# Other planner costs and thresholds for the modulation steps of a two-block kernel

## The chip, the cores and the metric

One Trainium2 chip, one core. The metric is the device time of one execution in microseconds (us). The engines are TensorE (PE, with its weight loads shown as PEld), VectorE (DVE), ScalarE (ACT), GpSimd (POOL) and SyncE (SP), which issues the transfers.

## The reference, cut to what matters

256 tokens of 1024 columns go through two blocks. The first mixes an mLSTM and a sparse attention (an indexer picks 64 keys for a query), with sigmoid and silu gates on the mLSTM's output, and ends in a gated residual and a norm. The second has two layers; the first layer's mixer is MLA attention, the second's is MoBA. Each layer is modulated by a small vector that depends on the input `c` alone:

```
c_act = silu(c)
mod = (c_act @ mod_w[i] + mod_b[i]).reshape(B, 6, D)[:, :, None, :]
hin = x * (1.0 + mod[:, 1]) + mod[:, 0]        # into the mixer
x = layer_norm(ALPHA * x + mod[:, 2] * y)
hin = x * (1.0 + mod[:, 4]) + mod[:, 3]        # into the feed-forward part
x = layer_norm(ALPHA * x + mod[:, 5] * y)
```

A product of one row with a 1024 x 1024 matrix per vector, six vectors for each layer. The vectors 0, 1, 3 and 4 of a layer are needed as columns, before the mixer (0, 1) and before the feed-forward part (3, 4). The vectors 2 and 5 are made on TensorE by other steps (`mod_k`).

## The kernel before

Weights stream from HBM in tiles of 128 x 1024 ("units", 512 KB). Each is split into a high and a low part: ScalarE rounds it (step `hi`), VectorE subtracts (step `lo`), and TensorE makes three products in place of one (lines 1291 to 1293). All engines work through one list of steps, each in the order of that list; an engine skips what isn't its own. The list is made by the function `order()` when the program is built.

`order()` keeps two clocks. `clock["pe"]` is the sum of `cost_pe` over the steps so far, and `clock["ve"]` is the end of VectorE's work, which never lies before the TensorE clock and grows by `cost_ve`. Their difference is called the backlog here: how far VectorE lags by the planner's own costs. The costs are numbers in a table, in units meant as microseconds.

The columns of the modulation come from a generator, `modulation()`. For each vector, in the order (0,0), (0,1), (0,3), (0,4) of the first layer (layer, vector), and then the same of the second, it gives these turns:

- eight steps `mod_v` (k from 0 to 7): a transfer of a 512 KB tile and a VectorE multiply and add over 128 x 1024 into an accumulator (lines 1612 and 1614)
- two turns that do nothing (one in the second layer)
- `mod_one`, eight short matmuls that sum over the partitions (line 1386), and `mod_sum`, a ScalarE copy of the sum from PSUM (line 2164)
- `mod_pe`, two transposes on TensorE (line 1395) that wait for `mod_sum`, and `mod_fin`, small VectorE operations (from line 1628)

So twelve turns make one vector. A turn is taken at the end of a weight unit, and between the heads of an attention that is being finished, where this holds:

```
t[2] = float(clock["ve"] - clock["pe"] < -t[1] and clock["pe"] - clock["mod"] > MOD_APART)
```

`-t[1]` is the threshold: `MOD_PACE[0]` in the first block, `MOD_PACE[1]` from the key and value projections of MLA on. `MOD_PACE[2:]` are positive and are rates, not thresholds; they hold after the first layer's MLA. What is missing when a vector is needed is placed at once, all in one go, by `until(i, m)` at the head of `modulated(...)`, which is called ahead of the transposes that feed a mixer or a feed-forward part.

Four stretches of the list matter here. The projections `w_aqk`, `w_av` and `w_az` (units with these names) run beside the mLSTM and the indexer. The projection `w_moz` (16 units) runs beside the sparse attention, whose steps are `sc` and `norm` with the task name "dsa" (lines 1804, 1823, 1826; TensorE's transposes of line 1471 wait for them); in it lie `gate_mo` (lines 1853 and 1859) and `ev_mz` (1866 and 1870). Then come `w_out`, `w_ple` and `w_gate`. Last, MLA: `mla_uv`, `mla_uk`, `mla_uq`, and `mla_o`.

The end of `mla_o` is the first layer's residual and layer norm. For each half t of the tokens VectorE adds and takes statistics (lines 1978 to 2010), POOL takes a power (2490), and ScalarE, with VectorE for a part of t = 1, scales (step `ln_fin`: lines 2350, 2356 and 2018). Then `modulated(0, 1)` is called: `until(0, 4)`, then five `mod_k` of another vector (line 1377), the transposes of t = 0 (1305), one `mod_k`, the transposes of t = 1, the scaling by the modulation's columns (1572 on VectorE, 2129 on ScalarE), and the feed-forward matmuls.

Of the kernel before, what the change touches and what calls it, by code (L numbers as in the profile page):

```python
# [20 lines left out]
CONST_AT, NCONST = spans(CONSTS)  # L21


MOD_PACE, MOD_APART = [-4.0, -5.0, 0.4, 0.5, 0.5], 2.0
LSTM_PACE, DSA_PACE, MLA_PACE, MOBA_PACE, GATES_PACE, INDEXER_PACE = 1.05, 1.53, 1.6, 0.87, 0.6, 0.8
SHARE = 0.65

# [30 lines left out]
def cost_ve(kind, a):  # L58

    wide = {"ix_s": 0, "ix_k": 0, "dist": 0}  # L60
    if kind in wide:
        return {"ix_s": 0.75, "ix_k": 1.5, "dist": 0.6}[kind] * (1.0 + 0.3 * a[0])
    if kind in ("lo", "hi") or kind in ("ev_mv", "ev_av", "ev_k", "ev_v", "ev_q"):
        return 0.0 if kind == "hi" or a[4 if kind in ("lo", "ev_v") else 2 if kind in ("ev_av", "ev_q") else 3] != "V" \
            else 1.2 if kind == "lo" else 0.65
    if kind in ("sc", "norm"):
        return 0.47 if of(a[0], a[1])[1] else 0.35
    if kind == "ml_s":
        return 0.95 if a[1] else 1.3
    if kind == "tab":  # L70
        return (0.6, 0.9, 1.5, 1.2, 1.9)[a[0]]
    return {"lo_half": 0.65, "xt_s": 0.9, "xt_hl": 0.65, "xf": 0.25, "xt_m": 1.0, "xt_lo": 0.65, "mod_v": 1.25,
            "mod_row": 0.4, "mod_pe": 0.2, "mod_fin": 0.6, "gev": 0.7, "gate": 0.55, "ix_f": 0.5, "conv": 2.7,
            "silu": 0.7, "ml_o": 0.5, "ev_az": 0.65, "fin_dsa": 1.1, "fin_o": 0.43, "ev_mz": 2.0, "gated": 1.7,
            "ev_wo": 0.65, "pt2": 0.65, "ev_gate": 1.3, "rms2_r": 0.5, "gain": 1.25, "res_m": 0.65, "res_a": 0.65,
            "res_s": 0.65, "ev_cq": 0.8, "rope": 0.85, "ffn_a": 1.8, "ffn_g": 0.65}.get(kind, 0.0)

# [22 lines left out]
def of(task, i):  # L100

    return (i // 4 * 2 + i % 2, i // 2 % 2) if task == "dsa" else (i // 2, i % 2)
# [42 lines left out]
def order():  # L145
# [5 lines left out]
    def add(*step):  # L151
        steps.append(step)
        clock["pe"] += cost_pe(step[0], step[1:])
        clock["ve"] = max(clock["ve"], clock["pe"]) + cost_ve(step[0], step[1:])
# [2544 lines left out]
```

## Time and profile before

| what | value |
| --- | --- |
| time, median of 3 runs | 877.66 us (877.63 to 877.71) |
| the profiled execution's own time | 876.84 us |
| its span, first to last instruction | 875.0 us |
| TensorE busy | 849.9 us, 97% |
| VectorE busy | 670.3 us, 77% |
| ScalarE busy | 457.8 us, 52% |
| mean granted TensorE clock | 0.998 |

Busy time is the union of an engine's instructions. A row of the timeline has the start, the length, the engine, the line, the operation and the tiles; in brackets, how long the engine had been idle before it, and what released it. The profiled execution took 0.82 us less than the median of the runs.

### The profile page before, as it was taken

Reading aid. Unit: us, or ns where it says so; the run is one execution under the profiler, and the core shown is the slowest. Engines: PE = TensorE matmul, PEld = TensorE weight load, DVE = VectorE, ACT = ScalarE, POOL = GpSimd, SP = SyncE. Lnnn points to the kernel's source line nnn. Section 1 sums busy time; section 2 is a strip of 40 time slices with the busy share of each in tenths; the row PEclk is TensorE's granted clock in tenths of the full one; section 3 lists DMA queues with packets and bytes.
Section 4 is the critical chain, followed back from the end, with each engine's and each line's share of the span. In section 5 each row is a group of like instructions: output and inputs, shape, how many; then the busy total and the mean of one; then the engine's idle time right before and its main releaser. Section 6 shows DMA issues by size and latency. Waiting matters only on the chain. (4 is left out here: it accounts for less than half of the span.)

```text
span 875.0 us, 14595 instructions
## 1 busy us (share of the span) xinstructions
PE 849.9 (97%) x5778; PEld 747.4 (85%) x5778; DVE 670.3 (77%) x1096; ACT 457.8 (52%) x737; POOL 81.4 (9%) x77
## 2 busy tenths in 40 slices
PE   9999999899999999999999999999999999999996
PEld 9989987677776987799999999689976999999995
DVE  6698798997887887799568767797777876566567
ACT  6564555554556545575544454365553854454450
POOL 1100004100001110012201000100000101001011
PEclk9999999999999999999999999999999999999999
DMA  9856654576885751989757796288617976646501
GB/s 336 308 178 222 197 210 148 201 243 217 310 337 190 292 197 35 403 318 360 263 164 270 284 366 201 95 289 336 220 69 302 328 292 198 209 146 201 185 1 49
DMA packets 56773, 200.61 MB, mean 229 GB/s; under 512 B 6585, under 2 KB 7793, under 8 KB 56705
## 3 DMA queue, kind: packets, MB, share of 16 engines
q1 hardware_dynamic: 55664, 196.43, 63.4%
q0 software_dynamic: 1040, 3.24, 1.2%
q8 instruction: 46, 0.75, 0.3%
q14 instruction: 23, 0.18, 0.1%
HBM read 198.50 MB, written 1.08 MB: 228 GB/s over the span
## 5 line engine op out<-in xcount | busy, mean ns | idle before, releaser
L1291 PE MATMUL ps<-XT,wsp 128*128 128x256 f32 x760 | 215.0, 283 | 2.2 <-issue 1.6
L1292 PE MATMUL ps<-XT,wsp 128*128 128x256 f32 x760 | 212.0, 279 | 0.0
L1293 PE MATMUL ps<-XT,wsp 128*128 128x256 f32 x760 | 211.9, 279 | 0.0
L1527 DVE TENSOR_TENSOR wsp<-ring,wsp 128x1024 fp32r<-128x1024 f32 x131 | 160.3, 1230 | 13.3 <-ACT wsp L2101 13.3
L2101 ACT CAST wsp<-ring 128x1024 fp32r<-128x1024 f32 x131 | 136.1, 1047 | 58.0 <-PE ps L1293 52.8
L1291 PEld LDWEIGHTS ps<-XT,wsp 128*128 128x128 f32 x760 | 142.7, 188 | 5.5 <-issue 3.6
L1292 PEld LDWEIGHTS ps<-XT,wsp 128*128 128x128 f32 x760 | 142.6, 188 | 0.5
L1293 PEld LDWEIGHTS ps<-XT,wsp 128*128 128x128 f32 x760 | 142.6, 188 | 0.0
L1291 PE MATMUL ps<-wsp,ra 128*128 128x512 f32 (+1 forms) x256 | 97.7, 382 | 2.9 <-DVE ra L1842 2.1
L1293 PE MATMUL ps<-wsp,ra 128*128 128x512 f32 (+1 forms) x256 | 97.2, 380 | 0.0
L1292 PE MATMUL ps<-wsp,ra 128*128 128x512 f32 (+1 forms) x256 | 96.6, 377 | 0.0
L1513 DVE SCALAR_TENSOR_TENSOR wk<-ps,cols,wk 128x255 f32<-128x255 f32 (+1 forms) x88 | 36.3, 475 | 70.9 <-ACT wk L2395 70.9
L1527 DVE TENSOR_TENSOR wsp<-arena,wsp 128x1024 fp32r<-128x1024 f32 x72 | 88.6, 1238 | 1.5 <-ACT wsp L2101 1.5
L2101 ACT CAST wsp<-arena 128x1024 fp32r<-128x1024 f32 x72 | 75.1, 1045 | 24.7 <-PE ps L1293 20.5
L1291 PE MATMUL ps<-XT,ra 128*128 128x256 f32 x288 | 81.3, 282 | 0.0
L1292 PE MATMUL ps<-XT,ra 128*128 128x256 f32 x288 | 80.7, 280 | 0.0
L1293 PE MATMUL ps<-XT,ra 128*128 128x256 f32 x288 | 80.7, 280 | 0.0
L1291 PE MATMUL ps<-wsp,XT 128*128 128x512 f32 x180 | 74.1, 412 | 3.6 <-issue 2.2
L1292 PE MATMUL ps<-wsp,XT 128*128 128x512 f32 x180 | 71.2, 396 | 0.0
L1293 PE MATMUL ps<-wsp,XT 128*128 128x512 f32 x180 | 71.1, 395 | 0.0
L2508 POOL TENSOR_TENSOR ra<-wk,ra 128x512 fp32r<-128x512 f32 x22 | 40.7, 1850 | 306.6 <-ACT ra L2408 306.6
L1291 PEld LDWEIGHTS ps<-wsp,ra 128*128 128x128 f32 x256 | 48.1, 188 | 15.0 <-DVE ra L1842 3.5
(276 smaller groups left out, 1538.3 us busy)
## 6 DMA issues: line engine op xcount, KB each, us to landing
ring<-in_mod_w SPq DMA_DIRECT2D x48, 512.0 KB, 4.8
arena<-in_mod_w SPq DMA_DIRECT2D x45, 512.0 KB, 6.5
ring<-in_ffn_o SPq DMA_DIRECT2D x29, 512.0 KB, 4.7
ring<-in_ffn_a SPq DMA_DIRECT2D x26, 512.0 KB, 4.7
arena<-in_ffn_b SPq DMA_DIRECT2D x25, 512.0 KB, 5.5
ring<-in_ffn_b SPq DMA_DIRECT2D x19, 512.0 KB, 4.9
arena<-in_ffn_a SPq DMA_DIRECT2D x18, 512.0 KB, 5.4
arena<-in_ffn_o SPq DMA_DIRECT2D x15, 512.0 KB, 5.1
```

Source lines behind the costliest of these rows:

```text
L1291: pe.matmul(o, l[0], r[0], start=start, stop=False)
L1292: pe.matmul(o, l[0], r[1], start=False, stop=False)
L1293: return pe.matmul(o, l[1], r[0], start=False, stop=stop)
L1513: ve.scalar_tensor_tensor(o[:, sh:256], src[:, q * 256:(q + 1) * 256 - sh], scale(tap, q), o[:, sh:256], MUL, ADD).then_inc(*done("V", top ...
L1527: ve.tensor_tensor(w[:, 1024:1024 + n], raw[slot[0]][:, 0:n], w[:, 0:n].bitcast(f32), SUB).then_inc(*done("V", "lo", u, also=[("raw", *slo ...
L2101: ac.copy(parts[p[0]][:, 0:n], raw[slot[0]][:, 0:n]).then_inc(*done("A", "hi", u))
L2508: po.tensor_tensor(gp[g[0]][:, 512:1024], wk[s[0]], gp[g[0]][:, 0:512].bitcast(f32), SUB).then_inc(*done("G", "ffn_lo", i, u, also=[("wk", ...
```

## The change

Two thresholds rise (from 4 to 5, and from 5 to 7), and entries of the planner's VectorE table change: `sc` and `norm` of the sparse attention cost 0.15 more each, `ev_mz` costs 1.4 in place of 2.0, and `gate_mo` costs 1.6. Until now `gate_mo` had no entry of its own, and cost 0: the entry stood under the name "gated", which no step bears. No instruction is added or removed; the order of the steps is what can change.

```
-MOD_PACE, MOD_APART = [-4.0, -5.0, 0.4, 0.5, 0.5], 2.0
+MOD_PACE, MOD_APART = [-5.0, -7.0, 0.4, 0.5, 0.5], 2.0
...
     if kind in ("sc", "norm"):
-        return 0.47 if of(a[0], a[1])[1] else 0.35
+        return (0.47 if of(a[0], a[1])[1] else 0.35) + (0.15 if a[0] == "dsa" else 0.0)
...
-            "silu": 0.7, "ml_o": 0.5, "ev_az": 0.65, "fin_dsa": 1.1, "fin_o": 0.43, "ev_mz": 2.0, "gated": 1.7,
+            "silu": 0.7, "ml_o": 0.5, "ev_az": 0.65, "fin_dsa": 1.1, "fin_o": 0.43, "ev_mz": 1.4, "gate_mo": 1.6,
```

## Rows read from the trace of the kernel before

**Rows 1.** The page, busy time by engine: us, share of span, instructions.

```profile
PE 849.9 (97%) x5778; PEld 747.4 (85%) x5778; DVE 670.3 (77%) x1096; ACT 457.8 (52%) x737; POOL 81.4 (9%) x77
```

**Rows 2.** Busy time in windows: PE, PEld, DVE, ACT, POOL, granted clock, DMA share, GB/s.

```profile
150.00:165.00 15.00, 14.16 (x77) 9.76 (x77) 14.28 (x30) 6.44 (x17) 2.41 (x4) 1.00 0.60 207
165.00:180.00 15.00, 12.89 (x71) 9.22 (x70) 13.47 (x33) 8.49 (x24) 1.48 (x2) 1.00 0.38 129
```

**Rows 3.** Timeline of TensorE, the rows before which it was idle, 100 to 240 us.

```profile
126.84 0.38 PE L1291 MATMUL ps<-XT,wsp 128*128 128x256 f32 x1 [0.58 <-DVE wsp L1527]
...
164.26 0.33 PE L1471 MATMUL ps<-cst,pb 128*128 128x128 f32 x1 [0.84 <-DVE pb L1826]
166.32 0.50 PE L1291 MATMUL ps<-wsp,XT 128*128 128x512 f32 x1 [0.32 <-DVE wk L1866]
169.61 0.33 PE L1471 MATMUL ps<-cst,pb 128*128 128x128 f32 x1 [1.04 <-DVE pb L1826]
175.91 0.70 PE L1457 MATMUL ps<-arena 64*128 64x256 f32 x4 [0.75 <-DVE ra L1564]
```

**Rows 4.** Timeline of VectorE, 113 to 177 us.

```profile
113.83 1.28 DVE L1614 SCALAR_TENSOR_TENSOR R<-ring,cactr,R 128x1024 f32<-128x1024 f32 x1
...
134.04 1.28 DVE L1614 SCALAR_TENSOR_TENSOR R<-ring,cactr,R 128x1024 f32<-128x1024 f32 x1
...
138.53 0.29 DVE L1804 CUSTOM_DVE_ANT_0 pb<-ps,arena 128x128 f32<-128x128 f32 x1 [2.01 <-POOL arena L2457]
...
146.49 0.17 DVE L1628 TENSOR_TENSOR small<-ps,cols 128x8 f32<-128x8 f32 x1 [0.75 <-PE ps L1395]
147.12 0.29 DVE L1804 CUSTOM_DVE_ANT_0 pb<-ps,arena 128x128 f32<-128x128 f32 x1 [0.47 <-PE ps L1457]
...
149.66 0.88 DVE L1859 SCALAR_TENSOR_TENSOR arena<-arena,small 128x256 f32<-128x256 f32 x2
...
162.11 1.27 DVE L1614 SCALAR_TENSOR_TENSOR R<-ring,cactr,R 128x1024 f32<-128x1024 f32 x1
...
176.81 1.28 DVE L1614 SCALAR_TENSOR_TENSOR R<-arena,cactr,R 128x1024 f32<-128x1024 f32 x1
```

**Rows 5.** Timeline of VectorE in MLA, 295 to 359 us.

```profile
295.23 1.28 DVE L1614 SCALAR_TENSOR_TENSOR R<-ring,cactr,R 128x1024 f32<-128x1024 f32 x1
303.43 0.42 DVE L2035 TENSOR_TENSOR wk<-ps,arena 128x256 f32<-128x256 f32 x1 [0.59 <-PE ps L1293]
304.87 0.42 DVE L2035 TENSOR_TENSOR wk<-ps,arena 128x256 f32<-128x256 f32 x1 [0.69 <-PE ps L1293]
...
345.40 0.42 DVE L1842 TENSOR_TENSOR ra<-ps,ra 128x256 fp32r<-128x256 f32 x1 [2.41 <-ACT ra L2291]
...
358.21 0.69 DVE L1978 TENSOR_TENSOR wk<-ps,R 128x512 f32<-128x512 f32 x1 [2.94 <-PE ps L1293]
```

**Rows 6.** Timeline of TensorE and ScalarE around the end of MLA, 354 to 369 us.

```profile
354.54 0.64 PE L1386 MATMUL ps<-R,cst 128*32 128x256 f32 x8
355.25 0.37 ACT L2164 COPY msum<-ps 128x256 f32<-128x256 f32 x1 [1.24 <-PE ps L1386]
...
360.80 0.38 PE L1395 MATMUL ps<-cst,msum 128*128 128x128 f32 x2
361.11 2.37 PE L1377 MATMUL ps<-arena,cactr 128*32 128x256 f32 x40
...
364.58 1.09 ACT L2356 ACTIVATE X<-X,small 128x256 f32<-128x256 f32 x2
...
365.00 1.27 PE L1305 MATMUL ps<-cst,X 128*128 128x128 f32 x8
365.99 0.56 ACT L2129 ACTIVATE wk<-ps,small 128x256 f32<-128x256 f32 x1 [0.32 <-DVE small L1649]
...
368.09 0.36 PE L1291 MATMUL ps<-XT,wsp 128*128 128x256 f32 x1 [0.81 <-issue]
```

**Rows 7.** Timeline of TensorE, its longest idle time inside the run.

```profile
266.38 1.09 PE L1305 MATMUL ps<-cst,X 128*128 128x128 f32 x8 [1.59 <-DVE X L1965]
```

**Rows 8.** Timeline of TensorE, the longest idle time in MLA's attention.

```profile
340.52 0.33 PE L1471 MATMUL ps<-cst,pb 128*128 128x128 f32 x1 [0.76 <-DVE pb L1826]
```

## The prediction

> **What bounds the kernel.** I read the page's busy times first: TensorE is busy for 849.9 of 875.0 us [rows 1], so about 25 us of idle time are all that an order of steps can win, and anything that stops TensorE is paid in full. Then the list of TensorE's idle rows, to see which of them the modulation's steps can reach. Up to the end of MLA (about 368 us) the change moves steps; behind it the thresholds are rates that stay as they are, and the list must come out the same. In the reachable part the idle rows are few: 0.58 us in `w_az`, and 0.84, 0.32, 1.04 and 0.75 us beside the sparse attention, 2.95 us in sum [rows 3]. There VectorE is the late one: it is busy 14.28 and 13.47 of 15 us in the windows that hold them, and TensorE 14.16 and 12.89 [rows 2]. The longest in MLA's attention is 0.76 us [rows 8]. So the most that could be won is some 3 to 4 us. Last I read the timeline around the end of MLA, because there the modulation's leftovers are placed in one go.
>
> **What the change moves.** The new table is nearer to the trace: `gate_mo` is one operation over 512 columns and two over 256, and the two alone take 0.88 us [rows 4], where the old table had 0. A higher cost in the sparse stretch and a higher threshold pull in opposite directions, so I followed the backlog by the planner's table: the old list gives the value (in the planner's units) at each chance, and I carried the differences.
>
> In `w_aqk` the chance at unit 4 had 4.18, and is now taken; the next one rises to 3.83 + 1.25 = 5.08 and is refused. From there the steps k = 5, 6, 7 of vector (0,0) come one chance earlier each, and the last one moves from the end of `w_az` to `w_av`. So (0,0) is finished one turn earlier, and the first three `mod_v` of (0,1) come at `w_moz` units 3, 4 and 5 in place of 4, 5 and 6. Then the new costs bite. The backlog at units 6 to 13 comes out as 5.99, 7.97, 7.30, 7.13, 6.11, 5.64, 6.53, 5.81, all over 5: no turn. Unit 14 has 4.81, one turn. The old list took eight `mod_v` of (0,1) in `w_moz`, the new one takes four. From `w_out` to `w_gate` all chances are taken in both lists. After `w_gate` the old list had seven `mod_v` of (0,3), the new one has three: it goes into MLA four turns late.
>
> In MLA the old list took 16 turns and left one (`mod_pe` with `mod_fin`) for `until(0, 4)`. The new one needs 21. With threshold 7 it takes 18: one old refusal (the spacing) is gone since `mod_one` now lies ahead of it, one with backlog 5.39 passes; the chance after `mla_o` unit 3 has 7.82 and is refused, and one stays refused for spacing. So three turns are left for `until(0, 4)`: a blank one, `mod_one` with `mod_sum`, and `mod_pe` with `mod_fin`. Two more turns would have to be found for `mod_one` to be placed in time, so this doesn't hang on one narrow comparison.
>
> **Cost at the end of MLA.** In the old list `mod_one` ran at 354.54 and ScalarE's copy at 355.25, six us ahead; `mod_pe` started at 360.80, directly behind the last matmul of `mla_o`, and from there TensorE went on without a gap: five `mod_k`, the transposes, the second half of them at 365.00 [rows 6]. In the new list `mod_one` stands behind that last matmul, and `mod_sum` stands on ScalarE behind `ln_fin` of both halves. The last of these ends at 364.58 + 1.09 = 365.67 [rows 6]. I take 0.5 us off, since `mod_one` (0.64) no longer lies ahead of the last matmuls, and VectorE waited for these (2.94 us idle) [rows 5, 6]: 365.2. The copy takes 0.37, so `mod_pe` starts at 365.6 in place of 360.80. Everything queued behind it on TensorE waits too, and it is just the work that used to fill the layer norm: 4.20 us from `mod_pe` to the second half of the transposes (365.00 less 360.80). These start at 369.8, the scaling some 0.6 us later at 370.4 against 365.99, so 4.4 us are lost, and the first feed-forward matmul goes from 368.09 to about 372.5. Nothing hides it: the whole of TensorE's queue stands behind `mod_pe`, and VectorE's and ScalarE's next steps behind the scaling. Bounds: 3.9 us if the scaling starts with the first pair of transposes at once, 5.3 us without the 0.5 and with the same distance of 0.99 us as before.
>
> **The other terms.** (1) `w_av` to `w_az`: one `mod_v` of 1.28 us more stands ahead of the low parts (113.83 and 134.04 are where the old k = 6 and 7 lie) [rows 4], and TensorE already waits 0.58 us for one of these [rows 3]. Between 0, if the small idle times of VectorE take it, and +1.28; I take +0.6. VectorE gets it back at 134, ahead of a wait of 2.01 us for POOL [rows 4], where less work is worth nothing. (2) The sparse stretch: up to 164 us VectorE has the same three `mod_v` ahead, a unit earlier each, which can only use its idle 0.75 + 0.47 us at 146 to 147 [rows 4]. The steps that leave the stretch are those from 176.81 on [rows 4], and behind 175.91 TensorE had no wait there [rows 3]: that relief comes too late. Gain between 0 and all 2.95 us; I take 1.0, near the idle time that can be used. (3) Early MLA: four `mod_v` (5.1 us) come in from 297 us on, and three leave by 317. VectorE had waited 0.59 and 0.69 us for TensorE there [rows 5], so it wasn't behind; the backlog reaches 4.3. Between 0 and +1.3 (5.1 less the 3.8 of the three that leave); I take +0.3. (4) Late MLA: three `mod_v` come in after `mla_o` unit 1, where VectorE has 2.41 and 2.94 us idle [rows 5]. Between 0 and +1.3, the first of them ahead of work that TensorE waits for; I take 0, since three times 1.28 are 3.8 us and the two idle times are 5.35. (5) `w_out` to `w_gate` has the same seven `mod_v` in both lists: 0. The transfers move with the `mod_v`, same count and bytes; no wait of TensorE in rows 3 is for one.
>
> Sum: 4.4 + 0.6 - 1.0 + 0.3 + 0 = +4.3 us. On the profiled execution that is 876.84 + 4.3 = 881.1 and a span of 879.3; the runs shown have a median 0.82 higher, so 877.66 + 4.3 = 882.0 us; I say 881.9.
>
> **The clock.** No row here has TensorE below its full granted clock: the windows have 1.00, and the longest idle time inside the run is 1.59 us [rows 2, 7]. The forecast makes a gap of 365.6 less about 361.0, that is 4.6 us, nearly three times that. If the clock fell to 1.2 GHz in it, the 4.20 us of matmuls and transposes behind it would take up to 4.2 us more. The Trainium skill says on the page "TensorE: Matmul & The Clock Gate", section "Part 1: The HAM clock gate (the "warmup" mystery)", that an idle array falls back to the half rate and needs sustained work to return; by that rule this gap is of the kind that can cost more than its length. The trace neither shows nor excludes it.
>
> **Rivals.** The clock falls in the new gap: up to 4.3 + 4.2, about 884 to 886.5 us. For it: such a gap is new here. Against: none in rows. Chance 0.07.
>
> MLA stalls as well: three more `mod_v` late in MLA and a backlog of 7.82 make the matmuls of `mla_o` wait. One late `mod_v` reaches TensorE twice, or the layer norm starts later by 1 to 3 us: 883.5 to 886. Against it: the idle 2.94 us just ahead of the norm [rows 5]. Chance 0.09.
>
> The end costs little: the copy doesn't wait for the norms, or `until(0, 4)` has only `mod_pe` left, as before. Then terms 1 to 4 alone are left, -0.1 us, and with a better half of the sparse stretch -1: 876.7 to 879.3, no change. Chance 0.11.
>
> Faster: the sparse stretch was bound by VectorE through the modulation, and pulling steps out of it takes away all 2.95 us and the 0.58 us in `w_az`, while the end costs nothing: 874.2 to 875.8. It decides only where at most `mod_pe` is left at the end, since 3.53 is less than 4.4. Chance 0.08.
>
> The forecast, +2 to +6: chance 0.65.
>
> **How the numbers follow.** 0.2% of the time, 1.75 us, is about what a measurement of this kernel can tell. Slower: 0.65 + 0.07 + 0.09 = 0.81, of which 0.01 may fall below the bound; same 0.11 + 0.01 = 0.12; faster 0.08. The range leaves out the faster case (0.08), part of the no-change one, and the upper part of the two dear ones: 878.4 to 884.8. The likeliest case's own range is 880 to 883.8.
>
> **What would show it.** In the changed kernel's trace: line 1386 with eight matmuls directly behind the last `mla_o` matmul, near 360 us; line 2164 on ScalarE behind line 2356's second group; an idle time of TensorE of 4 to 5 us before line 1395, ended by the copy; behind it the same distances as before. Beside the sparse attention only one row of line 1614 (or 1612) between 160 and 195 us, and idle rows of TensorE of about 2 us in sum in place of 2.95. Four more rows of line 1614 between 290 and 307 us. Behind 370 us, everything the same and later. It would be wrong if line 1386 stands inside `mla_o`, or if the idle rows of MLA's attention grow by over 1 us.

## The result, and the profile after

The changed kernel takes 883.72 us (median of 5 runs, 883.27 to 884.87), the kernel before 877.63 us beside it: a ratio of 1.0074, 95% interval 1.0062 to 1.0085, so slower by 6.1 us. The forecast was 881.9, range 878.4 to 884.8. The profiled execution took 883.27 us, the fastest of the five; its span is 881.4 us, 6.4 more than before.

The page's busy times are those of before [rows 1]: the same instructions, the same work.

```profile
PE 850.1 (96%) x5778; PEld 747.4 (85%) x5778; DVE 670.8 (76%) x1096; ACT 458.0 (52%) x737; POOL 79.1 (9%) x77
```

TensorE's idle rows up to the last projection of MLA, to be read against [rows 3, 7, 8]:

```profile
116.20 0.70 PE L1448 MATMUL ps<-arena,pb 128*128 128x257 f32 x2 [1.31 <-DVE pb L1773]
129.08 0.39 PE L1291 MATMUL ps<-XT,wsp 128*128 128x256 f32 x1 [0.47 <-DVE wsp L1527]
...
161.43 0.44 PE L1471 MATMUL ps<-cst,pb 128*128 128x128 f32 x2 [0.44 <-DVE pb L1826]
170.87 0.33 PE L1471 MATMUL ps<-cst,pb 128*128 128x128 f32 x1 [1.03 <-DVE pb L1826]
177.16 0.70 PE L1457 MATMUL ps<-arena 64*128 64x256 f32 x4 [0.74 <-DVE ra L1564]
...
309.18 0.49 PE L1464 MATMUL ps<-arena 128*128 128x128 f32 x2 [0.90 <-POOL arena L2502]
...
341.19 0.33 PE L1471 MATMUL ps<-cst,pb 128*128 128x128 f32 x1 [0.76 <-DVE pb L1826]
```

The differences here are small: beside the sparse attention the idle times add up to 2.21 us in place of 2.95, and there is one new wait of 1.31 us in the mLSTM's stretch and one of 0.90 us in early MLA. The end of MLA is another matter. The timeline of the same kernel, to be read against [rows 6]:

```profile
360.79 0.64 PE L1386 MATMUL ps<-R,cst 128*32 128x256 f32 x8
...
364.48 1.09 ACT L2356 ACTIVATE X<-X,small 128x256 f32<-128x256 f32 x2
365.47 0.35 ACT L2164 COPY msum<-ps 128x256 f32<-128x256 f32 x1
365.88 0.69 PE L1395 MATMUL ps<-cst,msum 128*128 128x128 f32 x2 [4.45 <-ACT msum L2164]
366.50 3.67 PE L1377 MATMUL ps<-arena,cactr 128*32 128x256 f32 x40
...
371.69 1.09 PE L1305 MATMUL ps<-cst,X 128*128 128x128 f32 x8
...
372.38 0.56 ACT L2129 ACTIVATE wk<-ps,small 128x256 f32<-128x256 f32 x1 [6.56 <-PE ps L1305]
...
374.48 0.36 PE L1291 MATMUL ps<-XT,wsp 128*128 128x256 f32 x1 [0.70 <-issue]
```

`mod_one` (1386) now stands behind the last matmul of `mla_o`, its copy (2164) behind the layer norm of both halves (2356), and TensorE idles 4.45 us before `mod_pe` (1395). Then comes what the forecast had only as a rival: the five `mod_k` take 3.67 us in place of 2.37, and the short transposes 0.69 in place of 0.38. The windows of 2 us of the changed kernel show why; the number behind the five busy times is the granted clock:

```profile
362.00:364.00 2.00, 0.00 (x0) 0.00 (x0) 1.52 (x5) 1.27 (x2) 0.45 (x1) 1.00 1.04 414
364.00:366.00 2.00, 0.12 (x1) 0.13 (x2) 0.73 (x2) 1.64 (x4) 0.11 (x1) 0.95 1.03 393
366.00:368.00 2.00, 2.00 (x18) 0.95 (x22) 0.84 (x5) 0.00 (x0) 0.00 (x0) 0.50 1.03 408
368.00:370.00 2.00, 2.00 (x28) 0.82 (x20) 0.00 (x0) 0.00 (x0) 0.00 (x0) 0.70 0.78 315
370.00:372.00 2.00, 2.00 (x23) 1.33 (x20) 0.00 (x0) 0.00 (x0) 0.00 (x0) 1.00 0.04 16
```

A granted clock of 0.50 is TensorE's lower level, 1.2 GHz. It fell while the engine stood idle, and was back when it had worked for some 3 us. All five executions of the changed kernel have a mean granted clock of 0.994 to 0.996, where the kernel before has 0.997 or more, which fits such a fall in each of them; only the profiled one shows where.

**Where the time went.** All kernels here run the same 1614 groups of three weight matmuls in the same order. So the start of the n-th matmul of line 1293 in one trace can be set against the n-th in another: the difference is how far a kernel lags. Worked out from the profiled executions (us, minus: ahead of before; the experiments are told below):

| kernel | at 48 | 130 | 187 | 302 | 349 | 372 | 867 us of before |
| --- | --- | --- | --- | --- | --- | --- | --- |
| changed | 0.46 | 2.24 | 1.23 | 0.39 | 0.66 | 6.39 | 6.39 |
| gap kept busy | 0.24 | 2.02 | 1.02 | 0.21 | 0.51 | 4.83 | 5.09 |
| mod_one hoisted | 0.22 | 1.94 | 0.83 | 0.00 | 0.27 | 0.42 | 0.56 |
| before, mod_one late | 0.38 | 0.31 | 0.19 | 0.25 | 0.27 | 7.13 | 7.46 |
| new thresholds alone | 0.41 | 2.21 | 6.56 | 5.56 | 5.79 | 4.81 | 4.96 |
| new costs alone | 0.24 | 0.31 | -0.92 | -2.29 | -1.89 | 6.53 | 6.45 |
| mod_pe behind the transposes | 0.15 | 1.97 | 1.00 | 0.21 | 0.50 | 1.56 | 1.79 |
| hoisted, 4 in w_aqk | 0.39 | 0.48 | 0.44 | -0.37 | -0.06 | 0.09 | 0.46 |
| none beside sparse | 0.59 | 2.46 | -0.80 | -2.86 | -0.66 | 5.48 | 5.54 |
| between the rows | 0.52 | 0.56 | -0.66 | -2.02 | -1.63 | -0.97 | -0.79 |

At 48 us no step has moved yet, and every kernel is 0.15 to 0.59 behind: the profiled execution of before had a lucky start (it was also 0.8 us under its median). With that taken off, the changed kernel has lost 0.66 - 0.46 = 0.2 us when the second half of `mla_o` begins. Between 349 and 372 us it loses 5.73 us, and from there to the end nothing. One thing to know when reading the table: while only one of two kernels has run a step that moved, the step itself shows as a lag; `mod_one` makes up to 0.8 us of it.

### The profile page after: what moved, and what is told of

Same layout as the page of the kernel before. It is cut to its first block and busy times, and to the rows that moved or that the text cites. A ratio compares the mean times of both kernels' runs of the same rounds, so it can differ in the third digit from the quotient of the medians.

```text
span 881.4 us, 14596 instructions
## 1 busy us (share of the span) xinstructions
PE 850.1 (96%) x5778; PEld 747.4 (85%) x5778; DVE 670.8 (76%) x1096; ACT 458.0 (52%) x737; POOL 79.1 (9%) x77
## 5 line engine op out<-in xcount | busy, mean ns | idle before, releaser
L1527 DVE TENSOR_TENSOR wsp<-ring,wsp 128x1024 fp32r<-128x1024 f32 x128 | 157.3, 1238 | 15.1 <-ACT wsp L2101 15.0
L2101 ACT CAST wsp<-ring 128x1024 fp32r<-128x1024 f32 x128 | 133.3, 1046 | 51.6 <-PE ps L1293 47.1
L2101 ACT CAST wsp<-arena 128x1024 fp32r<-128x1024 f32 x75 | 78.3, 1045 | 36.8 <-PE ps L1293 29.9
L1527 DVE TENSOR_TENSOR wsp<-arena,wsp 128x1024 fp32r<-128x1024 f32 x75 | 91.3, 1223 | 0.5 <-ACT wsp L2101 0.5
```

Source lines behind the costliest of these rows:

```text
L1527: ve.tensor_tensor(w[:, 1024:1024 + n], raw[slot[0]][:, 0:n], w[:, 0:n].bitcast(f32), SUB).then_inc(*done("V", "lo", u, also=[("raw", *slo ...
L2101: ac.copy(parts[p[0]][:, 0:n], raw[slot[0]][:, 0:n]).then_inc(*done("A", "hi", u))
```

## The experiments

**1. The gap kept busy.** The changed kernel, but the late `mod_one` writes its sums seven times over.

```
-                    for j in range(4):
+                    for j in list(range(4)) * (7 if (i, m) == (0, 4) else 1):
                         ins = pe.matmul(ps[b[0]][32 * j:32 * j + 32, 0:256], ones[:, 0:32],
```

> The changed kernel with the eight short matmuls of the late mod_one repeated seven times (same values written again), so that TensorE works through most of the 4.45 us in which it stood idle. Theory A (two costs at the end of MLA: the wait for ScalarE's copy, and the clock that falls in the gap): the wait stays, line 1395 starts as late as now, the granted clock stays at 1.00 and the 5.8 us from mod_pe to the second half of the transposes go back to 4.2, so the time falls by 1.6 us to about 882.1. Theory B (the work behind the gap is slow for another reason, the transfers or the row order): nothing but the repeated matmuls changes, 883.7 us or more.

Measured: 881.87 us, 1.0053 (1.0036 to 1.0070). Its timeline, and the window behind the gap:

```profile
360.63 3.23 PE L1386 MATMUL ps<-R,cst 128*32 128x256 f32 x56
365.72 0.44 PE L1395 MATMUL ps<-cst,msum 128*128 128x128 f32 x2 [1.86 <-ACT msum L2164]
366.09 2.37 PE L1377 MATMUL ps<-arena,cactr 128*32 128x256 f32 x40
...
369.98 1.09 PE L1305 MATMUL ps<-cst,X 128*128 128x128 f32 x8
```

```profile
366.00:368.00 2.00, 2.00 (x38) 1.20 (x40) 0.84 (x5) 0.00 (x0) 0.00 (x0) 1.00 1.02 403
```

`mod_pe` starts as late as in the changed kernel (365.72 against 365.88), but the five `mod_k` are back at 2.37 us, and from `mod_pe` to the second half of the transposes it takes 4.26 us in place of 5.81. More work for TensorE made the kernel faster, by 1.55 us there: the clock is a cost of its own, and the wait is the rest. Theory A. The trace carries this more than the times do: there are four executions, the intervals of the two kernels overlap, and one of the four took 883.65 us with a mean granted clock of 0.996 (the others 881.03 to 881.92 with 0.998), so the clock did not stay up every time.

**2. mod_one hoisted.** The changed kernel with two turns taken ahead of the last two units of `mla_o`.

```
         with_heads(0, mt)(cb, q)
+        if (cb, q) == (1, 2):
+            next(mod[0][0])
+            next(mod[0][0])
```

> The changed kernel with the blank turn and mod_one with mod_sum placed ahead of the last two units of mla_o, everything else as it is. Theory A (the loss is mod_one behind the last matmul): no wait for the copy, no fall of the clock, and the end of MLA as before the change; the time falls by 5.7 us to 878.0, that is 0.5 us above before, which is what the earlier moves lost. Theory B (the moved mod_v steps burden VectorE, and the late mod_one only shows where it falls behind): the layer norm ends later and half or less of the loss comes back, 880.5 us or more.

Measured: 877.41 us beside 877.48, ratio 1.0000 (0.9991 to 1.0010). All moved `mod_v` stand where the change put them, and the whole loss is gone; in the table the lag stays at 0.42 at 372 us. So the `mod_v` steps moved into late MLA cost nothing by themselves.

**3. Before, with mod_one late.** The opposite: the kernel before, no turn from the second half of `mla_o` on.

```
         with_heads(0, mt)(cb, q)
+        if (cb, q) == (1, 0):
+            mod[0][1] = 0
```

> The kernel before with one thing of the change: no turn from the second half of mla_o on, so that only mod_one with mod_sum (and blank turns) move behind the last matmul of mla_o. All mod_v stand where they stood. Theory A: this alone costs 5.7 us (4.1 of wait and 1.6 of clock), 883.3 us. Theory B (the loss comes from the mod_v steps moved into MLA): at most 1 us, 878.6.

Measured: 884.03 us, 1.0072 (1.0057 to 1.0087). This one displacement makes a loss as large as the whole of it. Timeline and windows of this kernel:

```profile
365.47 0.69 PE L1397 MATMUL ps<-cst,msum 128*128 128x128 f32 x2 [4.45 <-ACT msum L2166]
366.09 4.50 PE L1379 MATMUL ps<-arena,cactr 128*32 128x256 f32 x40
...
372.28 1.09 PE L1307 MATMUL ps<-cst,X 128*128 128x128 f32 x8
```

```profile
364.00:366.00 2.00, 0.53 (x2) 0.29 (x2) 0.48 (x2) 1.39 (x4) 0.00 (x0) 0.52 1.04 404
366.00:368.00 2.00, 2.00 (x21) 0.99 (x24) 0.84 (x5) 0.00 (x0) 0.00 (x0) 0.50 1.03 406
368.00:370.00 2.00, 2.00 (x28) 0.79 (x16) 0.00 (x0) 0.00 (x0) 0.00 (x0) 0.50 0.59 234
```

The gap is again 4.45 us, but the clock fell earlier in it (0.52 already in the window from 364) and stayed low for longer: 6.81 us from `mod_pe` to the second half of the transposes, where the changed kernel has 5.81. The price of the fall isn't fixed by the length of the gap; here it was 6.81 - 4.20 = 2.6 us. It is seen in one execution of each, and needn't be a difference between the kernels: their times overlap (883.22 to 884.29 us here, 883.27 to 884.87 for the changed kernel).

**4. New thresholds alone.** The kernel before with the old costs.

```
-MOD_PACE, MOD_APART = [-4.0, -5.0, 0.4, 0.5, 0.5], 2.0
+MOD_PACE, MOD_APART = [-5.0, -7.0, 0.4, 0.5, 0.5], 2.0
```

> The kernel before with the two thresholds raised (5 and 7) and the old costs. By the planner the turns then run ahead: mod_one of (0,4) falls after unit 1 of mla_o, and nothing is left for the end. Theory A: no gap at the end; what is left is the wait of 1.31 us in w_aqk, that both share, and more waits beside the sparse attention since mod_v comes in at w_moz 8 to 11, 0 to 3 us: 878 to 881. Rival: the higher thresholds are the cause of the loss whatever the costs, 883 or more. Rival: running ahead is free and early MLA gains, 877 or less.

Measured: 878.90 us (878.01 to 881.80 over 10 runs), 1.0020 (1.0011 to 1.0030); its profiled execution has a span of 880.0. It was the slowest of the ten; five took 878.01 to 878.57, with a mean granted clock of 0.997 in place of its 0.992. No gap at the end, as the planner said. But beside the sparse attention TensorE idles 0.45 + 0.69 + 0.32 + 1.04 + 0.38 + 1.51 = 4.39 us, and in the last of these the clock falls to 0.50, here too. Timeline and window of this kernel:

```profile
177.58 0.44 PE L1471 MATMUL ps<-cst,pb 128*128 128x128 f32 x2 [0.38 <-DVE pb L1826]
179.53 1.23 PE L1457 MATMUL ps<-arena 64*128 64x256 f32 x4 [1.51 <-DVE ra L1564]
180.69 0.79 PE L1291 MATMUL ps<-wsp,XT 128*128 128x512 f32 x1
181.28 0.63 PE L1292 MATMUL ps<-wsp,XT 128*128 128x512 f32 x1
```

```profile
178.00:180.00 2.00, 0.49 (x3) 0.50 (x4) 1.90 (x3) 1.77 (x4) 0.00 (x0) 0.81 0.35 139
180.00:182.00 2.00, 2.00 (x7) 1.16 (x5) 2.00 (x5) 0.04 (x1) 0.00 (x0) 0.50 0.18 18
```

The matmuls take 0.63 us in place of 0.39. The thresholds alone are not what cost the 6 us, but they aren't free: the median is 1.4 us above that of the kernel before. At 187 us this execution lags by 6.56, more than most of the ten lose in all.

**5. New costs alone.** The changed kernel with the old thresholds.

```
-MOD_PACE, MOD_APART = [-5.0, -7.0, 0.4, 0.5, 0.5], 2.0
+MOD_PACE, MOD_APART = [-4.0, -5.0, 0.4, 0.5, 0.5], 2.0
```

> The changed kernel with the old thresholds (4 and 5): the new costs alone. By the planner even mod_v k = 7 of (0,4) is then left for the end of MLA. Theory A (what is left for until(0, 4) sets the loss): mod_one waits for that mod_v (1.28 us), which stands behind VectorE's part of the layer norm, and the whole chain comes 1.3 to 2 us later than in the changed kernel, with at least the same fall of the clock; w_aqk has no wait of 1.3 us. 884.5 to 886.5. Rival (the higher threshold of MLA is at fault): less than the changed kernel, 882 or below.

Measured: 882.90 us, 1.0061 (1.0047 to 1.0074), between the two expectations. The end is as theory A has it, and dearer than in the changed kernel. Timeline of this kernel:

```profile
344.06 0.47 PE L1291 MATMUL ps<-wsp,ra 128*128 128x512 f32 x1 [0.29 <-DVE ra L1842]
...
362.29 1.28 DVE L1614 SCALAR_TENSOR_TENSOR R<-ring,cactr,R 128x1024 f32<-128x1024 f32 x1
363.62 1.08 PE L1386 MATMUL ps<-R,cst 128*32 128x256 f32 x8 [5.33 <-DVE R L1614]
364.77 0.37 ACT L2164 COPY msum<-ps 128x256 f32<-128x256 f32 x1 [1.71 <-PE ps L1386]
365.19 0.69 PE L1395 MATMUL ps<-cst,msum 128*128 128x128 f32 x2 [0.49 <-ACT msum L2164]
```

From 349 to 372 us it loses 6.53 + 1.89 = 8.4 us, against 5.73. What I had missed is that it comes to that place 1.9 us ahead of before (row at 344.06; the same one is at 345.97 in before). Beside the sparse attention only 1.03 and 0.76 us of idle time are left, and the wait in `w_aqk` isn't there. The new costs do what they are for, up to the end of MLA.

**6. mod_pe behind the transposes.** The changed kernel; of `until(0, 4)` only `mod_one` stays ahead of the `mod_k`, the rest moves directly ahead of the scaling.

```
                 add("tr", tag, k, (1,), banks[k], None)
+            if tag == "m01":
+                until(0, 4)
             split_pairs(tag, banks)
```

> The changed kernel, where of until(0, 4) only mod_one with mod_sum stands ahead of the mod_k and the transposes, and mod_pe with mod_fin stands behind them, directly ahead of the scaling. No step is earlier than now. Theory A (the loss is not the late mod_one but what is queued behind mod_pe on TensorE): the mod_k and transposes fill the time of the copy again, the clock stays, and the scaling starts about 1 to 1.5 us later than in the kernel before instead of 5.7: 879 to 879.6. Rival (the scaling needs mod_fin, and the copy is late anyway, so the order gains only the clock): 882.

Measured: 879.21 us, 1.0022 (1.0012 to 1.0031). Timeline of this kernel, with no idle row up to `mod_pe` (1401):

```profile
360.63 0.64 PE L1392 MATMUL ps<-R,cst 128*32 128x256 f32 x8
361.09 2.34 PE L1383 MATMUL ps<-arena,cactr 128*32 128x256 f32 x40
...
364.95 1.09 PE L1311 MATMUL ps<-cst,X 128*128 128x128 f32 x8
365.33 0.35 ACT L2170 COPY msum<-ps 128x256 f32<-128x256 f32 x1
365.88 0.38 PE L1401 MATMUL ps<-cst,msum 128*128 128x128 f32 x2
...
369.50 0.36 PE L1297 MATMUL ps<-XT,wsp 128*128 128x256 f32 x1 [2.23 <-issue]
```

No step is earlier than in the changed kernel, the copy is as late, and three quarters of the loss are gone. So most of the loss was what stood behind `mod_pe` in TensorE's queue, and the clock. What is left is TensorE's wait for the scaled columns, 2.23 us in place of the 0.81 of before: the scaling waits for `mod_fin`, so there the late `mod_pe` is still paid. The median lies between two groups, and that it fell into the expected 879 to 879.6 is luck: five of the ten executions took 878.37 to 878.63 us with a mean granted clock of 0.998, the other five 879.79 to 880.62 with 0.995 or 0.996. The profile is of the first group and has no fall of the clock; where it falls in the second, no trace shows.

**7. Hoisted, with threshold 4 in w_aqk.** As 2, with 4 up to `w_az` and 5 from `w_moz` on.

```
-    mod.append(W.beside(modulation(), MOD_PACE[0]))
+    mod.append(W.beside(modulation(), -4.0))
...
     add("ml_rs")
+    mod[0][1] = MOD_PACE[0]
```

> The kernel of the run that hoists mod_one ahead of the last units of mla_o, with threshold 4 as before in w_aqk, w_av and w_az, and 5 from w_moz on. Theory A (the wait of 1.33 us at 116 us is the higher threshold in w_aqk, and all of it is paid): the wait goes, the wait of 0.58 us in w_az comes back in place of 0.47, and the sparse stretch keeps two thirds of its relief: 876.2 to 876.8, faster than before by 0.1 to 0.2%. Rival (VectorE is late in the sparse stretch anyway and the saved time is lost there): 877.4.

Measured: 876.77 us, 0.9992 (0.9983 to 1.0001). The wait of 1.3 us at 116 is gone, the lag at 130 us falls from 1.94 to 0.48. Beside the sparse attention the idle rows are 0.82, 0.32, 1.03 and 0.77 us, those of before: I had expected two thirds of the relief there to stay, and none did. The 1.5 us won at 130 us are thus 0.6 us in the time (877.41 to 876.77 us, on different chips), and against the kernel before the gain isn't clear of the noise. The time lies in the expected range, 876.2 to 876.8, but the relief that the range counted on isn't there.

**8. No turn beside the sparse attention.** As 2 (all turns up to `mod_one` are hoisted), and no turns in `w_moz` from unit 3 to 13.

```
+        if (cb, q) == (0, 3):
+            mod[0][1] = 0
         gate_rows(0, cb, q)
...
+        if (cb, q) == (1, 2):
+            mod[0][1] = MOD_PACE[0]
         if (cb, q) == (0, 1):
             transposed("hm0", 4, None)
```

> The hoisted kernel with no turn at all from w_moz unit 3 to 13, so that no mod_v stands beside the sparse attention; the turns come later, and two mod_v and mod_one are placed in one go ahead of the last units of mla_o. What is asked is only TensorE's idle time between 150 and 180 us: it is 2.95 us before, 2.21 in the changed kernel, and 4.39 with the raised thresholds and old costs. Theory A (VectorE's load by mod_v makes these waits): 0.8 us or less. Rival (they belong to the attention's own chain from exp to norm): 2 us or more stay. The total is expected at 878 to 881, since mod_one then waits for VectorE.

Measured: one run, 882.40 us, above the 878 to 881 expected for the total. One idle row is left in the stretch, and then the price of putting everything off, at the hoisted `mod_one`:

```profile
175.13 0.70 PE L1467 MATMUL ps<-arena 64*128 64x256 f32 x4 [0.43 <-DVE ra L1574]
...
358.46 0.98 PE L1396 MATMUL ps<-R,cst 128*32 128x256 f32 x8 [4.52 <-DVE R L1624]
```

0.43 us with no `mod_v` from unit 3 on, 1.79 with the new costs alone, 2.21 in the changed kernel, 2.95 before, 4.39 with the thresholds alone: the waits are VectorE's load by `mod_v`. The clock fell twice in this run, behind the 4.52 us shown, and before that in the window from 316 us (0.92), behind an idle time of 1.36 us in MLA's attention.

**9. Between the rows.** New costs, thresholds 4 and 7 (`MOD_PACE = [-4.0, -7.0, ...]`), and what is left up to `mod_one` placed between the two last row steps of `mla_o`.

```
+    def amid_mla_o(cb, q):
+        while (cb, q) == (1, 2) and accs[1] != ("mod_one", 0, 4):
+            next(mod[0][0])
...
-    proj_a("ot0", 8, "mla_o", ..., True, before_mla_o)
+    proj_a("ot0", 8, "mla_o", ..., True, before_mla_o, amid_mla_o)
```

> New costs, thresholds 4 (as before) and 7, and what is left of mod_one placed between the two last row steps of mla_o, where VectorE is waiting for TensorE anyway. Up to the start of mla_o the run with the new costs alone stood 1.9 us ahead of the kernel before (344.06 against 345.97 us). Theory A (the new costs are right and what they put off needs only a place at the end of MLA that isn't behind the last matmul): the end of MLA is as before, no gap, clock 1.00, and the 1.9 us stay: 875.6 to 876.2. Rival (the put-off mod_v steps delay the layer norm once they stand directly ahead of it): 877.5 or more.

Measured: 875.57 us beside 877.47, 0.9977 (0.9968 to 0.9986): the fastest of all, and faster than before by 1.9 us. Timeline of this kernel:

```profile
356.11 0.64 PE L1390 MATMUL ps<-R,cst 128*32 128x256 f32 x8 [0.34 <-DVE R L1618]
```

`mod_one` waits 0.34 us for the last `mod_v`, and that is all that the end costs in waits; some 0.7 of the 1.63 us that it is ahead are lost there (table, 349 and 372 us).

## Why the prediction was right, and where a size was off

**The order.** The turns came out as worked out: steps (0,0) a chance earlier, three `mod_v` of (0,1) at units 3 to 5 and one at 14, three turns left for `until(0, 4)`. The direction hung on that: run 3 shows that this displacement alone is enough for the loss, run 2 that without it the other moves cost nothing that the times show. Two of the signs given with the forecast did not come out: between 290 and 307 us there are four rows of line 1614 in place of one, three more and not four (the next is at 308.8), and the distances behind the gap are not those of before.

**The end of MLA.** Forecast 4.4 us: `mod_pe` 4.8 us later, 4.20 us of queue, the scaling 0.6 behind the second half of the transposes. Measured with the 0.66 us of earlier lag taken off: `mod_pe` 365.88 - 360.80 - 0.66 = 4.42 later, the scaling 0.69 behind in place of 0.99. That makes 4.42 - 0.30 = 4.12. The step was right in its mechanism and within 0.3 us in size.

**The clock is the term that was mis-sized**: it stood at 0 in the sum, and as a rival with a chance of 0.07 and up to 4.2 us. It took 5.81 - 4.20 = 1.61 us, and the run with the busy gap gives 1.55 of it back. 4.12 + 1.61 = 5.73 is all that the table shows at this place. I had the gap at 4.6 us (measured 4.45), three times the longest of before, and still set the chance by the absence of such a row. The forecast says that the trace of before neither shows nor excludes a fall. That is wrong: it shows one, at its end, where TensorE has no work left. Its last matmul, and a window behind it:

```profile
866.96 0.28 PE L1293 MATMUL ps<-ra 128*128 128x256 f32 x1
```

```profile
870.00:875.00 5.00, 0.00 (x0) 0.00 (x0) 2.58 (x4) 0.00 (x0) 0.99 (x1) 0.57 0.28 105
```

TensorE's work ends at 867.24 us, and from 870 us on the mean granted clock is 0.57: it fell within some us of idleness, with nothing behind it that could be slowed. A forecast of a gap of 4.6 us should have given the fall far more than 0.07. That 883.72 us lies within the stated range all the same is in part luck: with the clock kept, run 1 takes 881.87, the forecast's own 881.9; with it fallen, the five executions reach 884.87, which is outside.

The page "TensorE: Matmul & The Clock Gate" of the Trainium skill, section "Part 1: The HAM clock gate (the "warmup" mystery)", says that an idle array drops to the lower rate. The traces agree, in the four kernels with a gap of over 4.4 us: the changed one, run 3, run 5 (5.33 us; granted clock 0.50 from 364 to 368 us) and run 8 (4.52 us; the weight matmuls behind it take 0.63 us in place of 0.39).

**The other terms** were forecast at 0.6 - 1.0 + 0.3 = -0.1 us in sum and came out at +0.2. That is near because their errors cancel: by the table they are 2.24 - 0.46 = +1.8 up to 130 us, 1.23 - 2.24 = -1.0 from there to 187, and 0.66 - 1.23 = -0.6 from there to 349. (1) `w_aqk` to `w_az`: 1.31 + 0.47 - 0.58 = +1.2 us in idle rows, at my upper bound, and by the table above it. The place is another too: not a low part was late but the mLSTM's `pb` (line 1773), which had one more `mod_v` ahead of it on VectorE and came at 115.86 us in place of 113.62. (2) The sparse stretch: 2.21 - 2.95 = -0.74, forecast -1.0. (3) Early MLA: +0.90 for a chain over POOL, and a wait of 0.47 us at 318 of before that is gone. (4) Late MLA: 0, as said.

**Not settled.** The idle rows don't add up to the table everywhere. From 187 to 302 us the changed kernel gains 0.8 us. Nearly all of it lies where the kernel before runs `mod_one` of (0,3), at 301.14 us, which the changed one runs at 316.55: the lag is 1.15 us at 298 and 0.40 at 304. But at 349 us, with that step done in both and 0.4 us more in idle rows since 187, the lag is only 0.66. Why the later place is the cheaper one stays open.

## What to carry to other kernels

A planner with a table of costs places work by the sum of all its entries: better costs held steps back where they hurt, and so pushed the remainder over a deadline that the table doesn't know. After changing a cost, look at what is left at each forced placement, not at the stretch the cost was for. And what matters most there is not the late step but what is queued behind its wait: three instructions that wait for another engine's copy belong behind the filler work (879.21 us in place of 883.72) or, better, ahead of the last long matmul steps (877.41).

## What the runs showed of the hardware

A gap of 4.45 us dropped the granted clock to 0.50 in both kernels that had exactly this gap, and cost 1.6 us in one and 2.6 in the other: it fell at another time in the gap. And it doesn't take one long gap. With the thresholds alone the clock fell in the second of two idle times, 0.38 and 1.51 us, with 0.44 us of work between them, and again in the window from 326 us after one of 1.56 us behind short matmuls; in experiment 8 it fell after one of 1.36 us. The 1.59 us of [rows 7], the 1.31 us of the changed kernel at 116 us, and 2.23 us in the profiled execution of experiment 6 left it at full level. The length of a gap alone doesn't sort these cases. With the thresholds alone ten executions spread over 3.8 us (878.01 to 881.80), and in experiment 6 over 2.3 us in two groups, the slower ones with the lower mean clock. Experiments 2, 7 and 9, with ten or eleven executions each and no fall of the clock in their traces while TensorE has work, spread over 0.7 to 1.3.
